# A ring of raw weights moved by 64 bytes in SBUF, in a kernel of four transformer layers

## The reference, cut to what matters

```python
y = conv_glu_ffn(h, w_up_act[l], w_up_lin[l], w_conv[l], b_conv[l], w_down[l])   # layers 0 and 1
def _swiglu(x, w_gate, w_up, w_down):                                            # layer 2
    return (jax.nn.silu(x @ w_gate) * (x @ w_up)) @ w_down
for e in range(N_EXPERTS):                                                       # layer 3
    out = out + combine[..., e:e + 1].astype(x.dtype) * _swiglu(x, w_gate[e], w_up[e], w_down[e])
```

## Time and profile before

| | |
|---|---|
| median of three runs | 2533.73 us |
| the profiled execution: its time, its span | 2533.41 us, 2531.6 us |
| mean granted TensorE clock | 0.976 |
| busy: PE, PEld, DVE, ACT, POOL | 95%, 78%, 68%, 49%, 26% of the span |
| HBM traffic | 650.06 MB, mean 257 GB/s |
| expert stage, about 1440 to 2520 us | PE at 100% in each full turn of 125 us |

### The profile page before, as it was taken

The page is one execution under the profiler, slowest core; times in us unless marked ns, Lnnn a source line. Parts: engine busy times, 40 slices in busy tenths (PEclk is TensorE's granted clock), DMA queues, the critical chain, the costliest instruction groups (busy, mean ns, idle before and its releaser), DMA issues. The chain is left out here.

```text
span 2531.6 us, 38194 instructions
## 1 busy us (share of the span) xinstructions
PE 2402.5 (95%) x15277; PEld 1971.8 (78%) x15277; DVE 1713.2 (68%) x2015; ACT 1231.7 (49%) x1317; POOL 649.2 (26%) x349
## 2 busy tenths in 40 slices
PE   6999999899999998999998789999999999999995
PEld 4875999885899775999876578888888888888773
DVE  2565677474876775665585697778787877776555
ACT  2344543443444223333213467676767676766451
POOL 0000000000940443940082123232323232232122
PEclk9999999899999998999999899999999999999998
DMA  9896864467784584785532489999999999998771
GB/s 338 276 351 216 273 210 156 149 203 253 243 254 156 189 277 150 237 245 184 168 100 99 141 310 332 352 356 350 355 350 356 349 352 354 349 357 315 250 272 44
DMA packets 416381, 650.06 MB, mean 257 GB/s; under 512 B 37018, under 2 KB 255222, under 8 KB 416246
## 3 DMA queue, kind: packets, MB, share of 16 engines
q1 hardware_dynamic: 389040, 633.12, 72.3%
q10 hardware_dynamic: 27206, 15.03, 2.1%
HBM read 647.06 MB, written 1.05 MB: 256 GB/s over the span
## 5 line engine op out<-in xcount | busy, mean ns | idle before, releaser
L1593 ACT ACTIVATE region_part<-ring 128x2048 fp32r<-128x2048 f32 x412 | 769.4, 1908 | 278.6 <-PE bank L874 204.5
L2584 DVE TENSOR_TENSOR ring_part<-ring,region_part 128x2048 fp32r<-128x2048 f32 x240 | 575.8, 2428 | 55.2 <-PE bank L1206 34.1
L874 PE MATMUL bank<-ring_part,region_part 128*128 128x512 f32 x1480 | 578.0, 391 | 0.0
L872 PE MATMUL bank<-region_part 128*128 128x512 f32 x1288 | 523.3, 406 | 11.6 <-DVE ring_part L2584 6.9
L873 PE MATMUL bank<-region_part 128*128 128x512 f32 x1152 | 449.9, 391 | 0.0
L1483 POOL TENSOR_TENSOR ring_part<-ring,region_part 128x2048 fp32r<-128x2048 f32 x48 | 248.2, 5178 | 514.8 <-ACT region_part L1593 428.2
L872 PE MATMUL bank<-xn_part,region_part 128*128 128x256 f32 x1152 | 331.0, 287 | 10.1 <-DVE hT_part L2222 8.1
L873 PE MATMUL bank<-xn_part,ring_part 128*128 128x256 f32 x1152 | 329.2, 286 | 0.0
L874 PE MATMUL bank<-hT_part,region_part 128*128 128x256 f32 x1152 | 329.0, 286 | 0.0
L874 PEld LDWEIGHTS bank<-ring_part,region_part 128*128 128x128 f32 x1480 | 278.2, 188 | 59.9
L872 PEld LDWEIGHTS bank<-region_part 128*128 128x128 f32 x1288 | 242.5, 188 | 77.2 <-issue 20.1
(11 more groups left out here) (379 smaller groups left out, 3905.5 us busy)
## 6 DMA issues: line engine op xcount, KB each, us to landing
ring<-in_moe_w_gate SPq DMA_DIRECT2D x112, 1024.0 KB, 5.1
ring<-in_moe_w_up SPq DMA_DIRECT2D x112, 1024.0 KB, 5.2
ring<-in_moe_w_down SPq DMA_DIRECT2D x112, 1024.0 KB, 4.9
ring<-in_w_ada SPq DMA_DIRECT2D x48, 1024.0 KB, 9.2
ring<-in_mod_w SPq DMA_DIRECT2D x48, 1024.0 KB, 7.0
ring<-in_w_in SPq DMA_DIRECT2D x44, 1024.0 KB, 5.6
ring<-in_w_up_act SPq DMA_DIRECT2D x22, 1024.0 KB, 5.5
ring<-in_w_up_lin SPq DMA_DIRECT2D x22, 1024.0 KB, 5.7
```

What stands on the lines that cost most here:

```text
L872: nc.tensor.matmul(o, split(a_hi), split(b_hi), start=start, stop=False, skip_group_check=True)
L874: return nc.tensor.matmul(o, split(a_hi), split(b_lo), start=False, stop=stop, skip_group_check=True)
L1593: return nc.scalar.activation(out_, in_, func, **kw).then_inc(*done(*event))
L2584: v.tensor_tensor(split(w), w, whole(hi), ALU.subtract).then_inc(*done("moe_lo", j, e))
```

## The change

Sixteen float32 (64 bytes in each partition) are put ahead of the ring, and the pad ahead of `region` grows by as much. No instruction is added, dropped or moved on any engine; the addresses alone differ.

```diff
     hT = sb_split("hT", KD * S).rearrange("p (k s) -> p k s", k=KD)
+    sb("ring_pad", 16)
     ring = sb_split("ring", SLOTS * SLOT)
...
     moe_pair = sb("moe_pair", 2 * NE * NE).rearrange("p (v a b) -> p v a b", v=2, a=NE)
-    sb("region_pad", 8)
+    sb("region_pad", 24)
     region = sb_split("region", REGION)
```

## The result

The changed kernel takes 2538.23 us (median of 17 runs, 2533.87 to 2540.42), the one before 2533.12 us over the 17 runs beside it (2531.13 to 2534.71). The ratio is 1.0019, with a 95% interval of 1.0012 to 1.0027. The profiled executions have spans of 2536.3 and 2531.6 us: +4.7 us. Forecast were 2545 us, so +11.6: the direction is right, the size more than twice the measured one.

A forecast was written before the change was run, and what follows sets the result against it. The prediction took the matrix engine as the bound: number of multiplications times the spacing of their starts. Its terms, +14.8 - 0.8 - 2.1 - 0.3 = +11.6 us on 2533.41 us, gave 2545 us, range 2523 to 2560 us.

The forecast's parts named there:

- experts: Expert loop: in 4032 multiplications stream and loaded matrix differ in phase; 4032 x 0.8 x 4.6 ns = +14.8 us.
- down: Down products: every group of three gets one mismatch; 152 `prow` groups go from 233.0 to 231.3 ns, -0.8 us.
- up: Up products, 256 columns: the held ring matrix leaves its stream's phase, one mismatch in three, -0.6 x 3456 = -2.1 us.
- input projection: Input projection: 256 groups get one mismatch, 128 go from two to one; -0.3 us, at most +5.3 us.
- VectorE, transfers: VectorE's subtraction stays at 2288 ns, and the DMA share of an expert turn stays under a turn: no cost.
- plain float32 and the rest: Plain float32 products that stream or hold the ring: no row shows both phases, taken as 0, within 5 us.
- the fifth that I left out: Expert loop: multiplications behind a transpose, put at a fifth, already run at about 230 ns and were not priced.
- thirty starts in 6.9 us: Expert loop, sign that the forecast is right: thirty starts span 6.9 us or more instead of 6.80.
- Faster: Expert loop, up and down: a mismatch lets stream and load pass each other; together -9.3, 2524 us, chance 0.20.
- No change: Down products are slow from straight code or busy engines, phases don't matter; 2533.5 us, within 4 us, chance 0.20.
- Only held matrices matter: Experts stay at 226.7 ns, down falls to it (-4.8), up pays (+15.9): +11.1, 2544.5 us, chance 0.12.
- Both: Experts +14.8 and up +15.9, down -0.8, input projection +1: 2564 us, chance 0.10.

The follow-up runs named there:

- e10: Against the kernel before, the ring moved by 64 bytes and `region` by 256, so the ring stands 64 ahead of it: 2538.2 us, ratio 1.0023.
- e4: Against the kernel before, the ring stays and everything behind it moves by 128 bytes: 2547.6 us, ratio 1.0060.
- e7: Against the kernel before, ring, `region` and the tiles between move by 64 bytes, `x`, `xn` and `hT` stay: 2522.0 us, ratio 0.9958.
- e15: Against the kernel before, a 64-byte pad between `xn` and `hT`, and `ffn_rows` and `prow` put at 192 modulo 256: 2521.6 us, ratio 0.9951.
- e11: As e7, with `ffn_rows` and `prow` put at 192 modulo 256 too: 2524.6 us, ratio 0.9964 against the kernel before.
- e2: Ring and `region` as in the changed kernel, the tiles between them moved by 64 bytes more: 2537.2 us, ratio 1.0020 against the kernel before.
- e3: Against the kernel before, every tile moves by 64 bytes, with a pad ahead of `x`: 2533.4 us, ratio 1.0005.
- e8: Against the kernel before, the tiles between ring and `region` (`ffn_rows`, `prow`) move by 64 bytes, `region` by 256: 2533.0 us, ratio 1.0002.

## Why the prediction was right and wrong

| term | forecast | measured | how |
|---|---|---|---|
| experts | +14.8 | +7.1 | stage 1077.2 to 1084.3 us |
| down | -0.8 | -1.2 | (230.4 - 231.8) x 864, unrounded |
| up | -2.1 | -1.9 | (119.4 - 119.9) x 3456, unrounded |
| input projection | -0.3 | -1.2 | (118.2 - 119.3) x 1152, unrounded |
| VectorE, transfers | 0 | 0 | 2288 ns; DMA share 0.97; no wait on a transfer |
| plain float32 and the rest | 0 | +1.9 | what is left of -2.4 us ahead of the experts |
| sum | +11.6 | +4.7 | spans |

**What held.** The bound (PE's spacing, in a loop without waits), the sign, the place (the experts lose, up and down gain a little), and the two zeros for VectorE and the transfers. By the forecast's own limit of 0.2%, 2528.7 to 2538.8 us, the measured 2538.2 counts as "same", to which it gave 0.26; the 17 runs on each side do tell it from no change. The +1.9 us left over can be nearly all the granted clock: 98.8 us at 1.2 GHz ahead of the experts against 95.2, at most half lost, so up to 1.8 us. It was not taken apart further.

**What was luck.** Up and down came within 0.4 us of their terms, but not by the reasons given. In down the `prow` groups were to gain 1.7 ns and the `region` groups nothing; they gained 1.2 (232.4 to 231.2) and 1.6 (231.2 to 229.6). In up one held matrix in three was to leave its stream. Modulo 256 all three did (`region` by 128, the ring by 64), and the stretches stand at 118.6 or at 119.9 ns, which only in the mean looks like a small gain; with the ring's move alone, e10, up gained 7.3 us.

**The step that failed** is the price of the expert term, 4.6 ns in "The nearest row is the down product with one mismatch in three, 231.3 - 226.7 = +4.6 ns", the carry-over from a held matrix to a stream that the prediction called the likeliest to fail. The loop measures 229.0 - 226.7 = 2.3 ns in its steady rows and 1.9 ns in the mean; 1.9 x 4032 = 7.7 us, and the stage shows 7.1. Of the 7.7 us the six slots make 1.6 x 3456 = 5.5; the other 2.1 (3.7 x 576) come from the seventh slot, where the prediction saw no more than the ring's mismatch. Neither the number of multiplications nor the fifth that I left out is to blame: with 1.9 in place of 4.6 x 0.8 = 3.7 ns the sum would have been +4.5 us and the forecast 2538 us.

Under it lies the wrong model that made the two rows look alike. That phase "is an address modulo 128 bytes" is refuted by e4. Modulo 256 it is not so that "872, 873 and all held matrices stay at 0": `region` goes from 128 to 0, and the ring comes to stand 64 *behind* it. Had the ring stood 64 ahead (e10), the same edit in the prediction's terms would have cost 17.6 us there, and 127.27 us a turn against the 127 I named. Even that nearness would have been luck: the price came from a pair at +64 (`ffn_rows` at 192, streams at 128), and e10's is at -64. A table of addresses modulo 256 stood ahead of the prediction, in one bracket; I priced both signs and both periods as one. The range of the term, -4.8 to +25.4, held all of them.

**What would show it.** Of the signs listed: thirty starts in 6.9 us (6.87, hit), 228, 229 and 236 in turn (228, 229, 230: the step of 236 never comes), a turn of 127 us (126.01), up at 119 to 120 (119.4), all down blocks alike near 231 (229.6 and 231.3; over all of them 228.9 to 231.6), 2288 ns (hit).

**The rivals.** *Faster* fails in the experts (229.6 ns, not 226.7 or less), but its idea is right at 256 columns, where any mismatch tried was at least as fast as agreement; e7 and e15 are that rival made real. *No change*: the interval of the ratio leaves out 1, and e11 takes away its reason. *Only held matrices matter* fails both ways: a ring that is only streamed costs the experts 1.6 (after, six slots) to 4.4 ns (e10), and up, which holds it, gains. *Both* fails as up doesn't pay. Over all layouts the expert loop runs at 227.7 to 233.3 ns, 22 us of time (stages of 1077.2 and 1099.7 us), with the same instructions.

**What stays open.** Why a group of three settles at a given pace. Most stretches run at the same pace in every layer of a layout, but not all: the third down block stands at 233.3 ns in layer 0 of before and at 228.9 in layer 1, and the second up stretch of e11 at 117.8 and 113.5. Layouts whose operands of a product stand alike differ too (up in after and e2, e7 and e11). So something beside the distances, perhaps how a stretch begins, has a part in it; no run isolated it. A single mismatch has no fixed price.

## What to carry to other kernels

Where the matrix engine is the bound and shows no wait, put the places of streamed and held operands side by side modulo 256 bytes, with the sign of their distance, before pricing a change of layout; in this kernel no mismatch beat agreement in the experts at 512 columns, and none lost to it in up at 256. A price read from one pair of operands doesn't carry over to another, nor to the opposite sign. A pad is one line and is cheap to try: read the spacing over thirty starts in each stage apart, as a gain in one stage can hide a loss in another, as in e10.

## What the runs showed of the hardware that was not expected

- The spacing of back-to-back multiplications depends on the distance, modulo 256 bytes, of the stream that runs and the matrix that is loaded: 226.7 ns in agreement, 228.7 to 233.3 ns in steady rows otherwise at 512 columns; 119.9 in agreement, 113.3 to 119.9 otherwise at 256. Moving everything by 64 bytes (e3), or one side by 256 (e6), leaves the time within 0.1%.
- A stretch of like multiplications falls into one of a few steady paces and stays in it: 113.3 or 117.8 ns in up for the same tiles, by turns from stretch to stretch (e7). Before had 119.7 to 120.3 in all its 36 stretches.
- The work of the other engines and of the transfers beside it left no mark on this spacing in down and up: 231.2 to 231.4 ns in down of e8 at DMA shares from 0.19 to full, 119.8 and 120.0 ns in up of before with all three engines at work or none.
- VectorE's subtraction (2288 ns) and the landing of a transfer (7.2 and 7.3 us for 512 KB) did not care about 64 bytes.
